# Two kinds of decode attention trade places in the mixer of a hybrid decoder step, and their cache loads with them

## The chip, the cores and the metric

The kernel runs on one core of a Trainium2 chip. The metric is device time in microseconds (us) of one launch; the number quoted is the median of the runs. The profile is one execution, recorded by the hardware profiler.

## What is computed

A two-layer decoder trunk, for a prompt of 256 tokens and, in the same launch, for 8 decode sequences of 8 new tokens each. In each layer a half-step SwiGLU FFN is followed by a mixer with three groups of heads (retention, dilated sliding window, differential attention), then cross-attention into 256 memory tokens, and a second FFN. Cut to what matters here:

```python
for l in range(DEPTH):                                     # 2 layers
    x = ffn_sublayer(x, ffn1_in[l], ffn1_out[l], ...)
    aq, ak, av, ag, bq, bk, bv, cq, ck, cv = project_mixers(x, w_in[l])
    o_a, st = retention(aq, ak, av, state_ret[:, l], pos, T)
    o_b = dilated_sample(bq, bk, bv, cache_win_k[:, l], cache_win_v[:, l], rel_bias[:, :H_B])
    past_k = cache_diff_k[page_table, l]                   # 8 pages of 128 tokens per sequence
    past_v = cache_diff_v[page_table, l]
    o_c = diff_attend(cq, concat(past_k, ck), concat(past_v, cv), pos, kpos, rel_bias[:, H_B:], lam)
    x = mixer_merge(x, o_a, ag, o_b, o_c, ...)
    x = cross_sublayer(x, cache_mem_k[:, l], cache_mem_v[:, l], ...)
    x = ffn_sublayer(x, ffn2_in[l], ffn2_out[l], ...)
```

The prompt goes through the same sublayers with its own keys and values. Differential attention forms `softmax(map 0) - lambda * softmax(map 1)`. The outputs of the window heads and of the differential heads do not depend on each other; both are needed by `mixer_merge`.

## The kernel before, in words

Everything is float32. The 320 tokens (256 prompt, 64 decode) are held with the features on the partitions. The large matmuls of the FFNs and projections run as three products each of high and low parts (lines 538 to 540 and 632 to 634); weights come through a ring of four 1 MB slots that GpSimd loads (line 485).

Attention in the mixer is a list of 16 **items**, `MIXER` (lines 54 and 55), which every engine walks in the same order. An item is one softmax: `diff_dec g` and `win_dec g` are the differential and the window heads of two decode sequences (pair g of four), `win_pro n` and `diff_pro n` are one prompt head. A decode item is always followed by a prompt item. Before, the list is `diff_dec 0, win_pro 0, ..., diff_dec 3, win_pro 3, win_dec 0, diff_pro 0, ..., win_dec 3, diff_pro 3`.

TensorE's function `attention` issues, for item i: the scores of item i+1, then the transposes of item i's probabilities (line 507), then the product with the values (`values`; line 798 for decode items). VectorE adds the bias and takes the maximum (line 1391), and scales by the sum (1428); ScalarE takes the exponential (1074) and copies the transposes out of PSUM (1084 to 1094). The scores of `diff_dec` are line 716, those of `win_dec` line 724, of the prompt items lines 732 and 733.

The cached keys and values of a decode item lie in the tile `cache`: slots 0 and 1 hold the keys of its two sequences, slots 2 and 3 the values. There is one such set, so a load waits until TensorE has used the last contents: keys wait for `s_psum` (the scores of the decode item before are done), values for `o_psum` (its value product is done). SyncE, SP in the profile, issues all of these loads in one program order (lines 365 to 467):

- A `diff_dec` item has 16 key pages and 16 value pages, each of 128 KB, each its own DMA at an address from the page table (line 378). The page numbers are first read into SP's registers (`page_numbers`, line 368).
- A `win_dec` item has two key loads and two value loads of 768 KB (line 400), a `cross_dec` item two and two of 1 MB.
- The loads of the first decode item wait only for the end of the first FFN (`w_used`), so they go out while the projections run; `cache` holds FFN weights until then.
- Behind the keys of the second decode item SP issues the outputs of the projections (`outputs_of_projections`, lines 425 and 427, 640 and 768 KB) and the load of the retention state (line 438, 1 MB).

`cache_in` makes TensorE wait for the pages: it counts the increments of `k_ready` and `v_ready`, of which there is one for each of the two sequences. After the mixer's items come retention, the output projection, the memory projections, cross-attention (items `CROSS`) and the second FFN.

Of the kernel before, what the change touches and what calls it, by code (L numbers as in the profile page):

```python
# [29 lines left out]
WK = 768  # L30
# [20 lines left out]

MIXER = ([item for i in range(4) for item in (("diff_dec", i), ("win_pro", i))]
         + [item for i in range(4) for item in (("win_dec", i), ("diff_pro", i))])
CROSS = ([("cross_dec", 0), ("cross_pro", 0)] + [("cross_dec", i) for i in (1, 2, 3)]
         + [("cross_pro", i) for i in (1, 2, 3)])
ITEMS = MIXER + CROSS
# [28 lines left out]
def build(nc, a, o):  # L87
    ctx = ExitStack()
    with ctx:
# [256 lines left out]
        def _(sp):  # L346
# [18 lines left out]
            with sp.Fori(0, L) as l:  # L365
# [14 lines left out]
                def after(kind, g):  # L380

                    return ITEMS.index((kind, g)) + 1
# [11 lines left out]

                def pair(name, used, before, g, ready, slot0, n):

                    sp.wait_ge(used.sem, used.upto(l, 0) + before)
                    for b2 in range(2):
                        src = a[name][bass.ds(l, 1), bass.ds(g * 2 + b2, 1)].rearrange("a b p c -> (a b p) c")
                        sp.dma_start(cache[:, slot0 + b2, 0:n], src).then_inc(ready[b2].sem, 16)  # L400


                def before_window(g):

                    return after("win_dec", g - 1) if g else after("diff_dec", 3)

                assert [after("cross_dec", g) for g in (1, 2)] == [len(MIXER) + 3, len(MIXER) + 4]

                def win_keys(g):
                    pair("wk", s_psum, before_window(g), g, k_ready, 0, 2 * WK)  # L410

                def win_values(g):
                    pair("wv", o_psum, before_window(g), g, v_ready, 2, 2 * WK)

                def cross_keys(g, before):
                    pair("ck", s_psum, before, g, k_ready, 0, 2048)
# [13 lines left out]
                numbers = [page_numbers(0)]  # L430

                wait_apart(sp, "sp", w_used.sem, w_used.upto(l, POS_FFN1 + FFN_SLOTS))
                diff_keys(numbers[0], 0)
                diff_values(numbers[0], 0)
                numbers += [page_numbers(1), page_numbers(2)]
                diff_keys(numbers[1], after("diff_dec", 0))
                outputs_of_projections()
                sp.dma_start(view(s_dec, [[1, 2048]]), layer_of(a["state"], l)).then_inc(st_in.sem, 16)
                diff_values(numbers[1], after("diff_dec", 0))
                diff_keys(numbers[2], after("diff_dec", 1))  # L440
                diff_values(numbers[2], after("diff_dec", 1))

                numbers.append(page_numbers(3))
                diff_keys(numbers[3], after("diff_dec", 2))
                diff_values(numbers[3], after("diff_dec", 2))
                for g in range(4):
                    win_keys(g)
                    win_values(g)
                cross_keys(0, after("win_dec", 3))
                cross_values(0, o_psum, after("win_dec", 3))  # L450
                wait_apart(sp, "sp", st_act.sem, st_act.upto(l, 1))
                sp.dma_start(layer_of(o["s_pro"], l), view(s_pro, [[1, 512]])).then_inc(out_st.sem, 16)
                sp.wait_ge(st_dve.sem, st_dve.upto(l, 4))
# [3 lines left out]
                sp.wait_ge(out_prj.sem, out_prj.upto(l, 32))  # L457
                sp.dma_start(memT, a["memT"]).then_inc(mem_in.sem, 16)
                cross_keys(1, after("cross_dec", 0))
                with sp.Fori(2, 4) as g:  # L460
                    cross_keys(g, g + (len(MIXER) + 1))
                    cross_values(g - 1, xv_psum, g - 1)
                cross_values(3, xv_psum, 3)
# [39 lines left out]
        def _(pe):  # L503
# [31 lines left out]
            with pe.Fori(0, L) as l:  # L535
# [158 lines left out]

                    return slice(64 * b2 + 32 * hp, 64 * b2 + 32 * hp + 32)

                def cache_in(ready, s, b2):

                    r = ready[b2]
                    pe.wait_ge(r.sem, r.upto(l, 16 * (NPG * min(s + 1, 4) + max(s - 3, 0))))  # L700

                def scores(i, first):
                    kind, n = ITEMS[i]
# [4 lines left out]
                    if kind == "diff_dec":  # L708
                        for c in range(3):
                            for b2, hp in QUARTERS:  # L710
                                if c == 0 and hp == 0:
                                    cache_in(k_ready, n, b2)
                                r = quarter(b2, hp)
                                rhs = (view(cache[:, b2, 1024 * c + 128 * hp:1024 * c + 128 * hp + 1], [[256, 4], [1, 128]])
                                       if c < 2 else fm[:, 6 + hp, SEQ:T])
                                last = mm(ps[r, b0 + c, 0:(512 if c < 2 else NS)],
                                          qd[:, hp, 2 * n + b2, 32 * hp:32 * hp + 32], rhs, start=True, stop=True)
                    elif kind == "win_dec":
                        for c, (at, w, bank, col) in enumerate(((0, 512, 0, 0), (512, 256, 1, 0), (0, NS, 1, 256))):
                            for b2, hp in QUARTERS:  # L720
                                if c == 0 and hp == 0:
                                    cache_in(k_ready, 4 + n, b2)
                                rhs = cache[:, b2, WK * hp + at:WK * hp + at + w] if c < 2 else fm[:, 2 + hp, SEQ:T]
                                last = mm(ps[quarter(b2, hp), b0 + bank, col:col + w], qw[:, hp, 2 * n + b2, :], rhs,
                                          start=True, stop=True)
# [8 lines left out]
                    elif kind == "cross_dec":  # L734
                        for c4 in range(4):
                            for b2, hp in QUARTERS:
                                if c4 == 0 and hp == 0:
                                    cache_in(k_ready, 8 + n, b2)
                                c = 4 * hp + c4
                                last = mm(ps[quarter(b2, hp), b0, 0:256], qc[:, c, 2 * n + b2, :],  # L740
                                          cache[:, b2, 256 * c:256 * c + 256], start=(c4 == 0), stop=(c4 == 3))
                    else:
                        for qb in range(2):
                            for c in (2 * n, 2 * n + 1):
                                last = mm(ps[:, b0, 256 * qb:256 * qb + 256], qxT[:, c, P * qb:P * qb + P], mkT[:, c, :],
                                          start=(c == 2 * n), stop=(c == 2 * n + 1))
# [33 lines left out]
                def values(i, first):  # L780
# [5 lines left out]
                    if kind in ("diff_dec", "win_dec"):  # L786
                        nk, v0 = (8, 256) if kind == "diff_dec" else (6, 0)
                        for k in range(nk + 1):
                            for b2, hp in QUARTERS:
                                if k == 0 and hp == 0:  # L790
                                    cache_in(v_ready, n if kind == "diff_dec" else 4 + n, b2)
                                r = quarter(b2, hp)
                                at = P * k + r.start
                                if k == nk:
# [14 lines left out]
                    elif kind == "cross_dec":  # L809
# [3 lines left out]
                        for kb in range(2):  # L813
                            for b2, hp in QUARTERS:
                                if kb == 0 and hp == 0:
                                    cache_in(v_ready, 8 + n, b2)
                                r = quarter(b2, hp)
                                last = mm(ps[r, bank, :], t[:, P * kb + r.start:P * kb + r.stop],  # L818
                                          cache[:, 2 + b2, 1024 * kb + 512 * hp:1024 * kb + 512 * hp + 512],
                                          start=(kb == 0), stop=(kb == 1))  # L820
# [982 lines left out]
```

## Time and profile before

| what | value |
|---|---|
| median of 3 runs | 2122.04 us (2118.92 to 2122.77) |
| the profiled execution's own time | 2125.29 us |
| its span in the profile | 2123.6 us |
| TensorE matmul busy | 1848.4 us (87%) |
| VectorE busy | 946.7 us (45%) |
| ScalarE busy | 670.3 us (32%) |
| mixer attention, layer 0, first scores to first retention transpose | 394.35 to 519.89 us |
| the same, layer 1 | 1435.57 to 1561.61 us |
| mean TensorE clock granted | 0.903 of full |

The table is read with care: TensorE's 87% is an average over FFN stages in which it never stops and attention stages in which it waits for other engines and for loads. What a change in the mixer is worth is read from the two stretches of 126 us, not from the averages.

### The profile page before, as it was taken

How to read it: one execution, taken by the hardware profiler on the slowest of the kernel's cores; microseconds unless marked ns; L12 is line 12 of the kernel's file. 1: busy time of each engine (PE TensorE's matmuls, PEld its weight loads, DVE VectorE, ACT ScalarE, POOL GpSimd, SP SyncE). 2: the span in 40 equal slices, each digit the busy share in tenths (PEclk: the TensorE clock that was granted, in tenths of full speed). 3: DMA queues.
4: the chain of work that ended last, by engine and by line, in shares of the span. 5: the costliest groups of instructions: out<-in, count | busy, mean ns of one | idle time of the engine just before them, and what ended most of it. 6: DMA issues, size and time to landing. Idle time of an engine off the chain costs nothing.

```text
span 2123.6 us, 31724 instructions
## 1 busy us (share of the span) xinstructions
PE 1848.4 (87%) x12214; PEld 1639.4 (77%) x12214; DVE 946.7 (45%) x1554; ACT 670.3 (32%) x913; POOL 114.9 (5%) x220
## 2 busy tenths in 40 slices
PE   4999999777898778999979999996788886799997
PEld 2999988535787457999969999883467773789997
DVE  3454353424454235544354543542346332545434
ACT  2333232322233124332243322432323331333323
POOL 0000100000000000000100001000000000000000
PEclk8999999866898998999979999996778988889998
DMA  5443463676143632443424434537733446224342
GB/s 176 140 157 118 147 212 130 210 234 228 65 149 108 242 116 80 157 139 129 155 91 142 158 119 162 187 127 246 249 144 106 139 139 238 80 100 151 133 137 80
DMA packets 84607, 319.51 MB, mean 150 GB/s; under 512 B 10138, under 2 KB 45338, under 8 KB 59402
## 3 DMA queue, kind: packets, MB, share of 16 engines
q0 software_dynamic: 31104, 205.53, 28.8%
q1 hardware_dynamic: 53386, 112.39, 15.3%
q8 instruction: 76, 1.25, 0.2%
q14 instruction: 41, 0.34, 0.1%
HBM read 307.10 MB, written 10.79 MB: 150 GB/s over the span
## 4 chain that ended last, share of the span: by engine, by line
PE 79%; DVE 6%; issue 4%; DMA 4%; SPq 3%; ACT 2%; DVEq 0%; ACTq 0%
PE ps L538 19%; PE ps L540 19%; PE ps L539 19%; PE ps L507 5%; SPq L378 3%; PE ps L632 3%; PE ps L634 3%; PE ps L633 3%; PE ps L798 2%; DMA cache<-in_cv 2%; DMA cache<-in_ck 2%; PE ps L740 1%; PE ps L818 1%; DVE bn L1279 1%; DMA hid<-bias_rows 1%
## 5 line engine op out<-in xcount | busy, mean ns | idle before, releaser
L538 PE MATMUL ps<-x_high,w_high 128*128 128x320 f32 x1408 | 439.7, 312 | 23.5 <-DVE w_low L1237 16.3
L539 PE MATMUL ps<-x_low,w_high 128*128 128x320 f32 x1408 | 438.8, 312 | 0.0
L540 PE MATMUL ps<-x_high,w_low 128*128 128x320 f32 x1408 | 438.6, 312 | 0.0
L985 ACT ACTIVATE w_high<-ring 128x2048 fp32r<-128x2048 f32 (+1 forms) x152 | 256.7, 1691 | 491.0 <-PE ps L540 478.6
L1237 DVE TENSOR_TENSOR w_low<-ring,w_high 128x2048 fp32r<-128x2048 f32 (+1 forms) x152 | 305.6, 2011 | 156.9 <-ACT w_high L985 156.6
L538 PEld LDWEIGHTS ps<-x_high,w_high 128*128 128x128 f32 x1408 | 267.9, 190 | 24.1 <-issue 24.1
L539 PEld LDWEIGHTS ps<-x_low,w_high 128*128 128x128 f32 x1408 | 267.9, 190 | 0.0
L540 PEld LDWEIGHTS ps<-x_high,w_low 128*128 128x128 f32 x1408 | 267.7, 190 | 0.0
L538 PE MATMUL ps<-h_high,w_high 128*128 128x320 f32 x704 | 219.9, 312 | 6.2 <-DVE h_low L1265 6.2
L1244 DVE TENSOR_TENSOR m_low<-ring,m_high 128x1024 fp32r<-128x1024 f32 x112 | 137.0, 1224 | 194.3 <-ACT m_high L1028 194.2
L485 POOL DMA_DIRECT2D ring<-in_w x216 | 114.7, 531 | 1970.7 <-PE ps L540 1769.3
L540 PE MATMUL ps<-h_high,w_low 128*128 128x320 f32 x704 | 217.5, 309 | 0.0
L539 PE MATMUL ps<-h_low,w_high 128*128 128x320 f32 x704 | 217.4, 309 | 0.0
L1028 ACT ACTIVATE m_high<-ring 128x1024 fp32r<-128x1024 f32 x112 | 118.3, 1060 | 296.5 <-PE ps L540 166.0
L1261 DVE TENSOR_TENSOR gate<-gate,ps 128x320 f32<-128x320 f32 x88 | 43.0, 489 | 274.7 <-PE ps L540 274.7
L538 PEld LDWEIGHTS ps<-h_high,w_high 128*128 128x128 f32 x704 | 132.2, 188 | 7.2 <-issue 7.2
L539 PEld LDWEIGHTS ps<-h_low,w_high 128*128 128x128 f32 x704 | 132.3, 188 | 0.0
L540 PEld LDWEIGHTS ps<-h_high,w_low 128*128 128x128 f32 x704 | 132.2, 188 | 0.0
L538 PE MATMUL ps<-x_high,m_high 128*128 128x320 f32 x384 | 126.2, 329 | 4.2 <-DVE x_low L1571 4.2
L539 PE MATMUL ps<-x_low,m_high 128*128 128x320 f32 x384 | 123.9, 323 | 0.0
L540 PE MATMUL ps<-x_high,m_low 128*128 128x320 f32 x384 | 123.6, 322 | 0.0
L507 PE MATMUL ps<-ident,tok 128*128 128x128 f32 (+1 forms) x228 | 69.0, 412 | 48.7 <-ACT tok L1042 31.5
(261 smaller groups left out, 2566.4 us busy)
## 6 DMA issues: line engine op xcount, KB each, us to landing
ring<-in_w POOLq DMA_DIRECT2D x152, 1024.0 KB, 5.2
ring<-in_w POOLq DMA_DIRECT2D x64, 704.0 KB, 4.3
cache<-in_dk SPq DMA_DIRECT2D x128, 128.0 KB, 2.3
cache<-in_dv SPq DMA_DIRECT2D x128, 128.0 KB, 2.8
cache<-in_ck SPq DMA_DIRECT2D x16, 1024.0 KB, 7.6
cache<-in_cv SPq DMA_DIRECT2D x16, 1024.0 KB, 7.5
cache<-in_wk SPq DMA_DIRECT2D x16, 768.0 KB, 7.3
cache<-in_wv SPq DMA_DIRECT2D x16, 768.0 KB, 5.0
```

The lines of the kernel that those rows point to most:

```text
L378: sp.dma_start(cache[:, slot0 + b2, 256 * pg:256 * pg + 256], src).then_inc(ready[b2].sem, 16)
L485: pool.dma_start(ring[:, r, 0:n], a[name][bass.ds(l * (a[name].shape[0] // L) + idx, 1)].rearrange("a p c -> (a p) c")).then_inc(w_ready[r ...
L507: return nc.tensor.transpose(out, in_, ident[0:in_.shape[0], 0:in_.shape[0]])
L538: mm(out, wh, xh, start=first, stop=False)
L539: mm(out, wh, xl, start=False, stop=False)
L540: return mm(out, wl, xh, start=False, stop=last)
L632: mm(out, xh, wh[:, c], start=first, stop=False)
L633: mm(out, xh, wl[:, c], start=False, stop=False)
L985: fn(w_high[:, pos % 2, 0:n], ring[:, pos % RING, 0:n], ACT.Copy).then_inc(hi_w.sem, 1)
L1028: fn(m_high[place][:, q % 2, :], ring[:, pos % RING, 1024 * (q % 2):1024 * (q % 2) + 1024], ACT.Copy)\
L1237: V.tensor_tensor(w_low[:, pos % 2, 0:n], ring[:, pos % RING, 0:n], w_high[:, pos % 2, 0:n].bitcast(F32), ALU.subtract).then_inc(lo_w.sem, 1)
L1244: V.tensor_tensor(m_low[place][:, q % 2, :], ring[:, pos % RING, 1024 * (q % 2):1024 * (q % 2) + 1024], m_high[place][:, q % 2, :].bitcast ...
```

## The change

The window items and the differential items trade places. Each decode kind now goes with its own prompt heads: `win_dec` with `win_pro` in the first half, `diff_dec` with `diff_pro` in the second. SP's loads follow: the window cache of pair 0 is loaded during the projections, and the pages of all four differential pairs come afterwards, each behind the use of the item before. The page numbers of pair g+1 are read ahead of the wait for the keys of pair g. In cross-attention a loop over two pairs on SP is written out.

```diff
-MIXER = ([item for i in range(4) for item in (("diff_dec", i), ("win_pro", i))]
-         + [item for i in range(4) for item in (("win_dec", i), ("diff_pro", i))])
+MIXER = ([item for i in range(4) for item in (("win_dec", i), ("win_pro", i))]
+         + [item for i in range(4) for item in (("diff_dec", i), ("diff_pro", i))])
...
                 def pair(name, used, before, g, ready, slot0, n):
-                    sp.wait_ge(used.sem, used.upto(l, 0) + before)
+                    if before:
+                        wait_apart(sp, "sp", used.sem, used.upto(l, before))
...
                 wait_apart(sp, "sp", w_used.sem, w_used.upto(l, POS_FFN1 + FFN_SLOTS))
-                diff_keys(numbers[0], 0)
-                diff_values(numbers[0], 0)
-                numbers += [page_numbers(1), page_numbers(2)]
-                diff_keys(numbers[1], after("diff_dec", 0))
+                win_keys(0, 0)
+                win_values(0, 0)
+                win_keys(1, after("win_dec", 0))
                 outputs_of_projections()
                 sp.dma_start(view(s_dec, [[1, 2048]]), layer_of(a["state"], l)).then_inc(st_in.sem, 16)
-                diff_values(numbers[1], after("diff_dec", 0))
-                diff_keys(numbers[2], after("diff_dec", 1))
-                diff_values(numbers[2], after("diff_dec", 1))
-
-                numbers.append(page_numbers(3))
-                diff_keys(numbers[3], after("diff_dec", 2))
-                diff_values(numbers[3], after("diff_dec", 2))
+                win_values(1, after("win_dec", 0))
+                for g in range(2, 4):
+                    win_keys(g, after("win_dec", g - 1))
+                    win_values(g, after("win_dec", g - 1))
                 for g in range(4):
-                    win_keys(g)
-                    win_values(g)
-                cross_keys(0, after("win_dec", 3))
-                cross_values(0, o_psum, after("win_dec", 3))
+                    if g < 3:
+                        numbers.append(page_numbers(g + 1))
+                    used = after("diff_dec", g - 1) if g else after("win_dec", 3)
+                    diff_keys(numbers[g], used)
+                    diff_values(numbers[g], used)
+                cross_keys(0, after("diff_dec", 3))
+                cross_values(0, o_psum, after("diff_dec", 3))
...
-                with sp.Fori(2, 4) as g:
+                for g in (2, 3):
                     cross_keys(g, g + (len(MIXER) + 1))
                     cross_values(g - 1, xv_psum, g - 1)
...
-                def cache_in(ready, s, b2):
-                    r = ready[b2]
-                    pe.wait_ge(r.sem, r.upto(l, 16 * (NPG * min(s + 1, 4) + max(s - 3, 0))))
+                def cache_in(ready, kind, n, b2):
+                    loads = {"win_dec": n + 1, "diff_dec": 4 + NPG * (n + 1), "cross_dec": 4 + 4 * NPG + n + 1}[kind]
+                    pe.wait_ge(ready[b2].sem, ready[b2].upto(l, 16 * loads))
```

How the instructions stand on SP where the mixer goes from its first half to its second (`in_dk` and `in_dv` are pages of keys and values, `in_wk` and `in_wv` the window cache; ISA rows set addresses). Before, from the last key page of pair 3 to the first window loads:

```order
L378 DMA cache<-in_dk 128x256
L378 DMA cache<-in_dv 128x256 [waits o_psum]
L378 DMA cache<-in_dv 128x256 x15
L397 REGISTER_ALU
L400 ISA [waits s_psum]
L400 DMA cache<-in_wk 128x1536
L400 ISA
L400 DMA cache<-in_wk 128x1536
L400 DMA cache<-in_wv 128x1536 [waits o_psum]
L400 DMA cache<-in_wv 128x1536
```

In the changed program, from the last window loads to the first key pages:

```order
L401 DMA cache<-in_wv 128x1536 [waits o_psum]
L401 DMA cache<-in_wv 128x1536
L368 TENSOR_LOAD pt x2
L331 REGISTER_ALU
L378 ISA [waits s_psum]
L378 DMA cache<-in_dk 128x256
L378 ISA
L378 DMA cache<-in_dk 128x256
```

All sixteen key pages of pair 0 now stand behind a wait for the scores of `win_dec 3`, and the reading of pair 1's page numbers stands ahead of them; before, only four large loads stood at this place.

TensorE at the same place (`qd` and `qw` are the queries of the differential and window decode heads, `arena` the transposed probabilities, `hid` here the new tokens' values, `fm` their keys). Before:

```order
L798 MATMUL ps<-cache,arena 32x128 x29
L798 MATMUL ps<-hid,arena 32x128 x4
L700 REGISTER_ALU [waits m_done]
L724 MATMUL ps<-cache,qw 32x512 [waits k_ready0]
L724 MATMUL ps<-cache,qw 32x512
L724 MATMUL ps<-cache,qw 32x512 [waits k_ready1]
```

Changed:

```order
L792 MATMUL ps<-cache,arena 32x128 x21
L792 MATMUL ps<-hid,arena 32x128 x4
L694 REGISTER_ALU [waits m_done]
L710 MATMUL ps<-cache,qd 32x512 [waits k_ready0]
L710 MATMUL ps<-cache,qd 32x512
L710 MATMUL ps<-cache,qd 32x512 [waits k_ready1]
```

The first scores of the second half now wait for pages (`k_ready`), where they waited for two window loads. Lines of TensorE's part stand six lower in the changed file.

## Rows read from the trace of the kernel before

**Rows 1.** The page, the chain that ended last: shares by engine and by line.

```profile
PE 79%; DVE 6%; issue 4%; DMA 4%; SPq 3%; ACT 2%; DVEq 0%; ACTq 0%
PE ps L538 19%; PE ps L540 19%; PE ps L539 19%; PE ps L507 5%; SPq L378 3%; PE ps L632 3%; PE ps L634 3%; PE ps L633 3%; PE ps L798 2%; DMA cache<-in_cv 2%; DMA cache<-in_ck 2%; PE ps L740 1%; PE ps L818 1%; DVE bn L1279 1%; DMA hid<-bias_rows 1%
```

**Rows 2.** Timeline of SP, layer 0: start us, us for the whole row, line, count.

```profile
284.27 9.79 SPq L378 DMA_DIRECT2D cache<-in_dk  x16
...
396.70 9.30 SPq L378 DMA_DIRECT2D cache<-in_dk  x16
...
409.76 9.84 SPq L378 DMA_DIRECT2D cache<-in_dv  x16
420.03 9.73 SPq L378 DMA_DIRECT2D cache<-in_dk  x16
429.94 7.45 SPq L378 DMA_DIRECT2D cache<-in_dv  x16
438.90 10.12 SPq L378 DMA_DIRECT2D cache<-in_dk  x16
...
501.92 0.81 SPq L400 DMA_DIRECT2D cache<-in_wv  x2
503.58 0.85 SPq L400 DMA_DIRECT2D cache<-in_ck  x2
```

**Rows 3.** Timeline of TensorE, layer 0: start, us, line, [idle before <-what ended it].

```profile
394.35 1.92 PE L716 MATMUL ps<-cache,qd 128*32 128x512 f32 x16 [2.17 <-DVE hid L1351]
...
409.48 1.93 PE L716 MATMUL ps<-cache,qd 128*32 128x512 f32 x14
...
431.78 2.77 PE L716 MATMUL ps<-cache,qd 128*32 128x512 f32 x10 [3.25 <-DMA cache<-in_dk]
...
448.87 1.77 PE L716 MATMUL ps<-cache,qd 128*32 128x512 f32 x4
450.84 1.48 PE L716 MATMUL ps<-cache,qd 128*32 128x512 f32 x10 [0.20 <-DMA cache<-in_dk]
...
466.11 2.12 PE L724 MATMUL ps<-cache,qw 128*32 128x512 f32 x16
...
501.77 1.50 PE L724 MATMUL ps<-cache,qw 128*32 128x512 f32 x16
...
519.89 0.48 PE L507 MATMUL ps<-ident,hid 128*128 128x128 f32 x1 [0.38 <-DVE tok L1464]
```

**Rows 4.** Timeline of SP, layer 1: its three key loads inside the mixer.

```profile
1438.56 8.82 SPq L378 DMA_DIRECT2D cache<-in_dk  x16
...
1461.05 10.39 SPq L378 DMA_DIRECT2D cache<-in_dk  x16
...
1480.57 10.24 SPq L378 DMA_DIRECT2D cache<-in_dk  x16
```

**Rows 5.** Timeline of TensorE, layer 1.

```profile
1435.57 2.48 PE L716 MATMUL ps<-cache,qd 128*32 128x512 f32 x16 [2.17 <-DVE hid L1351]
...
1507.95 1.74 PE L724 MATMUL ps<-cache,qw 128*32 128x512 f32 x16
...
1516.33 2.66 PE L798 MATMUL ps<-cache,arena 128*32 128x128 f32 x48 [0.63 <-ACT arena L1091]
...
1519.28 1.50 PE L724 MATMUL ps<-cache,qw 128*32 128x512 f32 x16
...
1543.18 1.69 PE L724 MATMUL ps<-cache,qw 128*32 128x512 f32 x12
...
1561.61 0.69 PE L507 MATMUL ps<-ident,hid 128*128 128x128 f32 x2 [0.39 <-DVE tok L1464]
```

**Rows 6.** Windows, layer 0: last three columns granted clock, DMA share, GB/s.

```profile
412.00:416.00 4.00, 2.14 (x11) 1.17 (x11) 2.80 (x9) 1.79 (x3) 0.00 (x0) 1.00 0.98 364
...
428.00:432.00 4.00, 0.75 (x8) 0.20 (x8) 0.00 (x0) 0.00 (x0) 0.00 (x0) 0.73 0.85 238
...
504.00:508.00 4.00, 2.53 (x20) 1.89 (x21) 2.82 (x14) 1.47 (x3) 0.00 (x0) 1.00 1.02 420
```

More of the change, by code:

```diff
@@ L400, in pair, with win_keys, win_values @@
                         sp.dma_start(cache[:, slot0 + b2, 0:n], src).then_inc(ready[b2].sem, 16)
[L403 to L413, printed above, removed]
+                def win_keys(g, before):
+                    pair("wk", s_psum, before, g, k_ready, 0, 2 * WK)
+                def win_values(g, before):
+                    pair("wv", o_psum, before, g, v_ready, 2, 2 * WK)
                 def cross_keys(g, before):
@@ L711, in scores @@
                                 if c == 0 and hp == 0:
-                                    cache_in(k_ready, n, b2)
+                                    cache_in(k_ready, kind, n, b2)
                                 r = quarter(b2, hp)
@@ L721, in scores @@
                                 if c == 0 and hp == 0:
-                                    cache_in(k_ready, 4 + n, b2)
+                                    cache_in(k_ready, kind, n, b2)
                                 rhs = cache[:, b2, WK * hp + at:WK * hp + at + w] if c < 2 else fm[:, 2 + hp, SEQ:T]
@@ L737, in scores @@
                                 if c4 == 0 and hp == 0:
-                                    cache_in(k_ready, 8 + n, b2)
+                                    cache_in(k_ready, kind, n, b2)
                                 c = 4 * hp + c4
@@ L790, in values @@
                                 if k == 0 and hp == 0:
-                                    cache_in(v_ready, n if kind == "diff_dec" else 4 + n, b2)
+                                    cache_in(v_ready, kind, n, b2)
                                 r = quarter(b2, hp)
@@ L815, in values @@
                                 if kb == 0 and hp == 0:
-                                    cache_in(v_ready, 8 + n, b2)
+                                    cache_in(v_ready, kind, n, b2)
                                 r = quarter(b2, hp)
```

## The prediction, made before the changed kernel ran

> **What bounds the kernel now.** I read the chain of waits first [rows 1]: 79% of it is TensorE, nearly all in the FFN and projection lines 538 to 540 and 632 to 634, which the change doesn't touch. The page loads stand in it as SP's own issue, line 378, with 3%. So the question is confined to the two stretches of mixer attention, of which I read SP's timeline beside TensorE's.
>
> Layer 0's stretch lasts from 394.35 to 519.89, 125.54 us; layer 1's from 1435.57 to 1561.61, 126.04 us; mean 125.8 [rows 3, 5]. I call the start of a decode item's scores S, and the moment at which TensorE may go on because the second sequence's key pages are in, R.
>
> In the first half SP is the bound. It issues the 16 value pages of one pair in 7.45 us, then the 16 key pages of the next in about 10, and 2.0 us after the last key page TensorE goes on: keys end at 420.03 + 9.73 = 429.76, R is 431.78, after an idle time of 3.25 us [rows 2, 3]. The next R comes 19.06 us later, at 450.84. The same item with little stall needs 450.84 to 466.11, 15.27 us, to the next decode item. In the second half a window pair lasts (501.77 - 466.11) / 3 = 11.89 us in layer 0 and (1543.18 - 1507.95) / 3 = 11.74 us in layer 1 [rows 3, 5], and there the bound is the walk from score to maximum, exponential, transposes, copies and values, since four large loads take SP only about 1.7 us a pair (two of them 0.81 us) [rows 2].
>
> One point matters more than the rest: pair 0's pages were loaded at 284.27, 110 us before their use [rows 2]. Only three of four differential pairs waited.
>
> **The change part by part.** *Removed and added work:* none on TensorE, VectorE or ScalarE; the items are the same sixteen in another order. SP's loads are the same too. The written-out loop in cross-attention removes a branch that stands between loads and waits for TensorE; I cost it at nothing, hidden by those waits, and at 1 us in all if it were not.
>
> *Window pairs first.* The pair that follows a window *prompt* item is the one in layer 1 that takes 1519.28 - 1507.95 = 11.33 us [rows 5]; later ones, behind a differential prompt item with twice the maxima and exponentials, take about 0.4 more. All window pairs now have that neighbour: 3 x 11.33 = 34.0 us. Ends: 33.5 (the first pair has nothing before it) and 35.7 (3 x 11.89).
>
> *From the last window scores to the first R.* SP issues the last window values 0.15 us after S and takes 0.81 [rows 2, 3]. Then come page numbers: where SP read them between values and keys, the gap is 438.90 - (429.94 + 7.45) = 1.51 us [rows 2]. Then 16 key pages; the six such rows inside the mixer are 9.30, 9.73, 10.12, 8.82, 10.39 and 10.24, mean 9.77 [rows 2, 4]; then 2.02 us to land. 0.15 + 0.81 + 1.51 + 9.77 + 2.02 = 14.3 us. The wait for `s_psum` of `win_dec 3` is over before: the loads behind it went out at S + 1.81 (503.58) [rows 2, 3]. This load was covered, and is not any more; TensorE would have been ready after 11.33, so 2.9 us of stall are new.
>
> *R to R.* The values wait for the product before, which is done by then, so SP runs through: 0.18 us gap (429.76 to 429.94), values 7.45, numbers 1.51, keys 9.77, in all 18.9 us, twice (pairs 1 and 2). For pair 3 no numbers are read and the gap is 0.43 (419.60 to 420.03), 17.8 us. TensorE needs 15.27, or 448.87 - 431.78 = 17.09 where the stall before left its clock low (0.73 mean granted in that window, levels 1.2 and 2.4 GHz) [rows 3, 6]; both lie under 17.8, so SP stays the bound and the low clock is hidden, except in the last pair. The value load of 9.84 us at 409.76 is the far end; I take 7.45, because the slow one ran beside the projections' outputs and the state load, which now go out in the window half.
>
> *Last R to the end.* 15.27 for the last differential pair, and what a last pair costs over a middle one: 519.89 - 501.77 - 11.89 = 6.2 in layer 0, 1561.61 - 1543.18 - 11.74 = 6.7 in layer 1, taken as 6.45. Together 21.7 us; with a low clock 23.5.
>
> *Weighing a rule on size.* Sixteen pages of 128 KB are issued in 8.8 to 10.4 us and land 2 us later, at 238 GB/s [rows 2, 4, 6]. The Trainium skill, "DMA: Bandwidth & Descriptors", section Bandwidth, puts a 64 KB transfer at 0.95 us and asks for 1 MiB per DMA; taken as one page after the other, 16 pages would need over 15.2 us, and the now exposed loads would cost some 45 us more in each layer. The trace disagrees: the pages overlap.
>
> **The sum**, for one layer: 34.0 + 14.3 + 37.8 + 17.8 + 21.7 = 125.6 us, against 125.8. That is -0.2 a layer, -0.4 in all. The profiled execution took 2125.29 us and would take 2124.9. The median of the runs, 2122.04, lies 3.25 under it, so I predict **2121.6 us**. The new stall of pair 0 (2.9) and page numbers read inside two more gaps are paid for by the window pairs' shorter walk, by value pages that no longer share the queue with 2.5 MB of outputs and state (2.4 us of issue), and by the end.
>
> Below about 0.2%, 4.2 us, a measurement of this kernel can't tell from no change.
>
> **The rivals.**
>
> *The keys go out faster (faster).* If all four key loads take 8.82 us, as the quickest row [rows 4], instead of 9.77, each layer gains 3.8 us: 2121.6 - 7.6 = 2114.0. For it: both quick rows, 8.82 and 9.30, had no value load right before them, and pair 0's keys won't either. Against: pairs 1 to 3 do have one, and such rows are 9.73 to 10.39. Under 8.82 nothing in the trace reaches. It counts as faster when the mean falls below about 9.3.
>
> *The lost cover is not given back (slower).* SP's first 32 page loads leave the projections for a place where TensorE waits for them, the window pairs stay at 11.8 (+1.4 a layer), and keys behind values take 10.39 (+2.5): 125.6 + 3.9 = 129.5, 3.7 over before in each layer, 2129.4. For it: three of the four rows behind values are above 10. Against: the 11.33 row, and the quick rows for pair 0. It decides when the two together cost over 2.3 us a layer. The Trainium skill says the same of such a move in "DMA: Bandwidth & Descriptors", Rules for kernel authors: issue a DMA early, compute, and wait for it late. By that rule the group with most DMAs should keep the early place; the trace agrees as far as pair 0 of before shows no wait.
>
> *The window half starves (slower).* Behind `win_dec 1`'s keys SP now has outputs and state in its queue, and the window values behind them. From about 396.1 that is 1.57 + 2.49 + 1.57 = 5.6 MB, needed 8.4 us after the second S (1516.33 - 1507.95) [rows 5], at 394.35 + 11.33 + 8.4 = 414.1. At the 238 GB/s of page traffic it would be 5.7 us late, 2121.6 + 11.4 = 2133.0 for both layers; it decides below 5.6 / 18.0 = 313 GB/s. Large loads moved 420 GB/s and the mixed traffic with outputs in it 364 [rows 6], so it is unlikely; loads of weights still running at the start speak for it.
>
> That the change does nothing is excluded: the order shown above has it on every engine.
>
> **How the numbers follow.** No change 0.64, keys faster 0.16, lost cover 0.12, starving 0.08. Only these give the chances: faster 0.16, same 0.64, slower 0.20. The range reaches from the quick keys' 2114 to just over the lost cover, 2130; it leaves out the starving case, and value loads that all stay at 9.84 (+14.3). The forecast's own range is 2118 to 2126, which holds the ends of the window pairs, a low clock in the last pair (+1.8 a layer), and keys half way to either end.
>
> **What would show it.** Right: in the changed profile the first window pairs 11.3 to 11.5 us apart with no wait for `in_wk` or `in_wv`; the first `diff_dec` scores with a wait for `in_dk` of about 3 us, R's 18.9, 18.9 and 17.8 apart; four waits for keys a layer where there were three; SP's line 378 still in the chain, and with more than 3%. From the last window scores to the end it is 91.6 us, against 34.0 before them. Wrong: key rows far from 9.8; a value load over 8 us in the differential half; a wait for a window load; R to R set by TensorE and not by SP; any change outside the two stretches above 1 us, since I cost everything there at nothing.

## The result, and the profile after

The changed kernel takes 2132.08 us (median of 6 runs, 2127.56 to 2134.16), the kernel before on the same chip 2120.88 (6 runs, 2118.92 to 2126.08). The ratio is 1.0036, with a 95% interval from 1.0023 to 1.0050: slower by 5 to 11 us, where 2121.6 had been predicted. The two medians themselves lie 11.2 us apart, a ratio of 1.0053, so the size of the loss is less sure than the interval says. A later repetition of both gave 1.0025 (1.0013 to 1.0037) and 2131.51 against 2125.72, 5.8 us. By the two ratios the loss is 5 to 8 us, and I reckon with that.

The profiled execution took 2133.52 us, its span is 2131.8. Page of the changed kernel, busy times, then the chain by engine and line, then two rows of its DMA issues (count, KB each, us to landing):

```profile
PE 1853.9 (87%) x12214; PEld 1640.3 (77%) x12214; DVE 947.1 (44%) x1554; ACT 670.5 (31%) x913; POOL 114.4 (5%) x220
...
PE 78%; DVE 6%; SPq 5%; DMA 5%; issue 4%; ACT 2%; DVEq 0%; ACTq 0%
PE ps L532 19%; PE ps L534 19%; PE ps L533 19%; PE ps L501 5%; SPq L378 4%; PE ps L626 3%; PE ps L627 3%; PE ps L628 3%; DMA cache<-in_ck 2%; PE ps L792 1%; PE ps L734 1%; DMA cache<-in_cv 1%; DVE bn L1273 1%; PE ps L812 1%; DMA hid<-bias_rows 1%
...
cache<-in_dk SPq DMA_DIRECT2D x128, 128.0 KB, 2.4
cache<-in_dv SPq DMA_DIRECT2D x128, 128.0 KB, 2.4
```

The work is the same as before; what grew in the chain is SP's own issue, from 3% to 5%, line 378 within it from 3% to 4% [rows 1].

Timeline of SP, changed kernel, layer 0. These rows answer to [rows 2]:

```profile
401.93 1.39 SPq L432 DMA_DIRECT2D s_dec<-in_state  x1
408.82 1.73 SPq L401 DMA_DIRECT2D cache<-in_wv  x2
...
432.85 0.81 SPq L401 DMA_DIRECT2D cache<-in_wv  x2
435.21 10.19 SPq L378 DMA_DIRECT2D cache<-in_dk  x16
445.58 7.45 SPq L378 DMA_DIRECT2D cache<-in_dv  x16
454.53 9.97 SPq L378 DMA_DIRECT2D cache<-in_dk  x16
464.68 7.45 SPq L378 DMA_DIRECT2D cache<-in_dv  x16
473.64 9.89 SPq L378 DMA_DIRECT2D cache<-in_dk  x16
483.71 7.75 SPq L378 DMA_DIRECT2D cache<-in_dv  x16
491.84 9.18 SPq L378 DMA_DIRECT2D cache<-in_dk  x16
```

Timeline of TensorE in the same stretch, for [rows 3]; line 718 is the window scores, 710 the differential ones:

```profile
396.75 1.50 PE L718 MATMUL ps<-cache,qw 128*32 128x512 f32 x16 [2.14 <-DVE hid L1345]
...
432.59 1.50 PE L718 MATMUL ps<-cache,qw 128*32 128x512 f32 x16
...
444.22 1.86 PE L710 MATMUL ps<-cache,qd 128*32 128x512 f32 x4
447.26 1.48 PE L710 MATMUL ps<-cache,qd 128*32 128x512 f32 x10 [1.18 <-DMA cache<-in_dk]
...
466.26 2.71 PE L710 MATMUL ps<-cache,qd 128*32 128x512 f32 x10 [2.86 <-DMA cache<-in_dk]
...
485.34 1.48 PE L710 MATMUL ps<-cache,qd 128*32 128x512 f32 x10 [0.98 <-DMA cache<-in_dk]
...
502.89 1.48 PE L710 MATMUL ps<-cache,qd 128*32 128x512 f32 x10 [1.67 <-DMA cache<-in_dk]
...
523.28 1.97 PE L501 MATMUL ps<-ident,hid 128*128 128x128 f32 x8 [0.39 <-DVE tok L1458]
```

In layer 0 all four differential pairs now wait for keys, with SP running through from 435.21 to the end. Before, only two pairs did, not three as the prediction says: pair 1's scores start at 409.48 without a wait [rows 3]. What came late for that pair were its values (kernel before, TensorE, layer 0):

```profile
422.63 3.63 PE L798 MATMUL ps<-cache,arena 128*32 128x128 f32 x60 [0.95 <-DMA cache<-in_dv]
```

In layer 1 of the changed kernel three pairs show such a wait. There is also one that before did not have, for window keys (for [rows 5]):

```profile
1438.05 1.74 PE L718 MATMUL ps<-cache,qw 128*32 128x512 f32 x16 [2.17 <-DVE hid L1345]
...
1460.84 1.05 PE L718 MATMUL ps<-cache,qw 128*32 128x512 f32 x4 [0.55 <-DMA cache<-in_wk]
1462.90 1.80 PE L718 MATMUL ps<-cache,qw 128*32 128x512 f32 x8 [1.01 <-DMA cache<-in_wk]
...
1476.19 1.73 PE L718 MATMUL ps<-cache,qw 128*32 128x512 f32 x16
...
1490.61 2.78 PE L710 MATMUL ps<-cache,qd 128*32 128x512 f32 x10 [2.07 <-DMA cache<-in_dk]
...
1567.58 1.97 PE L501 MATMUL ps<-ident,hid 128*128 128x128 f32 x8 [0.39 <-DVE tok L1458]
```

The repetition has no wait for window keys in either layer, so this one belongs to a single execution. It also shows three waits for keys in each layer.

Where the time went, by stages, from the first and last rows of each stage (us; "mixer" is first scores to first retention transpose, "rest" from there to the first cross-attention scores: retention, output projection, memory projections). Under each kernel stands a second profiled execution with the same mixer, from the runs below:

| | mixer 0 | mixer 1 | rest 0 | rest 1 |
|---|---|---|---|---|
| before | 125.54 | 126.04 | 178.65 | 178.04 |
| before, cross loop written out | 125.32 | 122.19 | 178.52 | 178.38 |
| changed | 126.53 | 129.53 | 177.70 | 177.88 |
| changed, repeated | 126.85 | 128.52 | 178.32 | 179.63 |

The four mixers of before average 124.8 us, the four of the changed kernel 127.9: 3.1 a layer, 6.2 in all, which lies between the 5.3 and 7.6 us of the two ratios. Everything else stays within what two executions of one kernel differ by. In the first pair of profiles another 4.7 us lie at the two ends of the launch (first FFN matmul at 47.29 instead of 44.83, and the second layer's last FFN 2.3 longer). The repetition starts at 44.94 and takes 307.44 us for that last FFN; before has 44.83 and 307.40. So that part belongs to the execution and not to the change.

### The profile page after: what moved, and what is told of

Its sections match the earlier page's. It is cut to its first block, busy times and chain, and to the rows that moved or that the text cites. A ratio compares the mean times of both kernels' runs of the same rounds, so it can differ in the third digit from the quotient of the medians.

```text
span 2131.8 us, 31734 instructions
## 1 busy us (share of the span) xinstructions
PE 1853.9 (87%) x12214; PEld 1640.3 (77%) x12214; DVE 947.1 (44%) x1554; ACT 670.5 (31%) x913; POOL 114.4 (5%) x220
## 4 chain that ended last, share of the span: by engine, by line
PE 78%; DVE 6%; SPq 5%; DMA 5%; issue 4%; ACT 2%; DVEq 0%; ACTq 0%
PE ps L532 19%; PE ps L534 19%; PE ps L533 19%; PE ps L501 5%; SPq L378 4%; PE ps L626 3%; PE ps L627 3%; PE ps L628 3%; DMA cache<-in_ck 2%; PE ps L792 1%; PE ps L734 1%; DMA cache<-in_cv 1%; DVE bn L1273 1%; PE ps L812 1%; DMA hid<-bias_rows 1%
## 5 line engine op out<-in xcount | busy, mean ns | idle before, releaser
L532 PE MATMUL ps<-x_high,w_high 128*128 128x320 f32 x1408 | 440.1, 313 | 23.9 <-DVE w_low L1231 16.7
```

Source lines behind the costliest of these rows:

```text
L532: mm(out, wh, xh, start=first, stop=False)
```

## The experiments

In each the ratio is to the kernel before on the same chip, with its 95% interval. A "mixer" figure is the mean of the two layers' stretches in that run's profile.

**1. Is the written-out cross loop free?** The kernel before with this alone:

```diff
-                with sp.Fori(2, 4) as g:
+                for g in (2, 3):
```

> The kernel before, with only the loop over pairs 2 and 3 of SP's cross-attention loads written out. Theory A (the loss arises in the mixer, from the page loads and the window half): no difference from the kernel before, within 2 us, and cross-attention, from its first scores to its last value product on cached values, stays at 51.2 to 51.9 us. Theory B (the written-out loop is a part of the loss, by its longer straight code on SP): 2 to 5 us slower than before, with later issues of in_ck or in_cv in cross-attention.

Measured 0.9994 (0.9984 to 1.0004), 2124.79 us against 2124.74. It costs at most 1 us, so the loss lies in the order and the loads that go with it. Layer 1's mixer, 122.19 against 126.04 in the kernel before, shows that one and the same mixer spreads by 4 us between layers and executions, so one profile is a weak base for a few microseconds.

**2. The changed kernel once more, and with the outputs out of the window half.** The state load moves with the outputs behind the last value pages:

```diff
-                outputs_of_projections()
-                sp.dma_start(view(s_dec, [[1, 2048]]), layer_of(a["state"], l)).then_inc(st_in.sem, 16)
                 win_values(1, after("win_dec", 0))
...
                     diff_values(numbers[g], used)
+                outputs_of_projections()
+                sp.dma_start(view(s_dec, [[1, 2048]]), layer_of(a["state"], l)).then_inc(st_in.sem, 16)
                 cross_keys(0, after("diff_dec", 3))
```

> The changed kernel, with the outputs of the projections and the state load moved from behind the second window keys to behind the last value pages. Theory A (in the changed kernel the window half starves behind these 2.5 MB, 2.6 us in the profiled layer 1): no wait for in_wk in either layer, window half 35.5 to 36 us in both, 2 to 5 us faster than the changed kernel. Theory C (the starving is a chance of one execution, and the loss is the page loads that are no longer covered): within 1.5 us of the changed kernel.

> The changed kernel once more, for a second profile and to be timed on one chip with the next two. If the starving of the window half is part of what the change does (theory A): a wait for in_wk of 1 to 3 us in at least one of the two layers again, window halves of 36 to 38 us, mixers of 126 to 130 us, and a ratio to the kernel before of 1.002 to 1.005. If it was a chance of one execution (theory C): no such wait.

> e2 once more, beside the changed kernel on the same chip. Theory A (outputs and state ahead of the window loads cost time): 3 to 6 us faster than e9, and no wait for in_wk in either layer. Theory C: within 1.5 us of e9; the difference between e2 and the changed kernel was one between two sets of runs.

Outputs late: 1.0007 (0.9995 to 1.0020), and on the second chip 1.0016 (1.0002 to 1.0029), where the changed kernel had 1.0025 (1.0013 to 1.0037). The intervals overlap, so a gain in time is not shown. What moved inside is clearer. Windows over the first to the fourth window scores, changed kernel; last three columns granted clock, DMA share, GB/s:

```profile
396.75:432.59 35.84, 25.21 (x288) 15.49 (x288) 11.45 (x46) 10.25 (x29) 0.00 (x0) 0.76 0.84 318
1438.05:1476.19 38.14, 27.01 (x288) 15.58 (x288) 11.44 (x46) 10.26 (x29) 0.00 (x0) 0.74 0.80 299
```

The same with outputs late:

```profile
396.43:432.07 35.64, 25.82 (x287) 15.47 (x288) 11.44 (x46) 10.27 (x29) 0.00 (x0) 0.71 0.66 250
1441.13:1475.69 34.56, 24.76 (x288) 14.93 (x288) 11.44 (x46) 10.27 (x29) 0.00 (x0) 0.76 0.69 257
```

Over both executions of each, the three pairs take 35.84, 38.14, 35.43, 36.48 (mean 36.5) with the outputs among them and 35.64, 34.56, 35.59, 34.90 (mean 35.2) without. So outputs and state load cost about 1.3 us a layer there. It is a rough figure: half of it is the one stretch of 38.14 us with the wait for window keys, and without that one the changed kernel's mean is 35.9. The mixer as a whole did not gain: 127.9 and 127.8 against 127.9, because the differential half behind it took 1.4 us longer, above all its last pair (mean of four 24.7, against 23.2). That is where the transfers were moved to, but TensorE shows no wait for them there, so why it is longer is open.

**3. Neighbours alone.** The order of the decode kinds as before, but each with its own prompt heads:

```diff
-MIXER = ([item for i in range(4) for item in (("diff_dec", i), ("win_pro", i))]
-         + [item for i in range(4) for item in (("win_dec", i), ("diff_pro", i))])
+MIXER = ([item for i in range(4) for item in (("diff_dec", i), ("diff_pro", i))]
+         + [item for i in range(4) for item in (("win_dec", i), ("win_pro", i))])
```

> The kernel before, with the differential decode heads still first and their page loads unchanged, but each kind beside its own prompt heads (diff_dec with diff_pro, then win_dec with win_pro). Theory A (the neighbour costs or gives nothing; what counts is which pages have cover): within 2 us of the kernel before, window pairs 11.8 to 12.0 us as with either neighbour. My prediction's term (a window pair is 11.33 us beside window prompt heads): window pairs 11.3 to 11.5, and 2 to 4 us faster than before.

> e3 once more. If matching neighbours give their gain in the mixer: mixers of 120 to 122.5 us again, against 122 to 126 of the two profiles with crossed neighbours, and 9 to 12 us faster than the kernel before. If the gain in the mixer was a chance of the granted clock: a mixer over 124 us in one layer at least, and a smaller gain in time.

Measured 0.9945 (0.9931 to 0.9959) and 0.9960 (0.9942 to 0.9979): 8 to 12 us faster than the kernel before. Expected were 2 to 4 us, if anything. Two gains of like size make this up. The mixers take 121.4 and 122.1, some 3 us less a layer: the differential half lasts as long as before although its prompt items are the heavier ones (72.35 and 70.03 us here, 71.76 and 72.38 before), since SP's issue sets it, and the window half's pairs carry the lighter ones. The second gain lies where nothing was edited, in the stage behind the mixer (175.6 to 175.9 instead of 178.0 to 178.7). Windows over the output and memory projections, layer 0, of the kernel before, of the changed kernel and of this one:

```profile
563.70:698.50 134.80, 122.11 (x720) 112.03 (x720) 61.57 (x72) 46.84 (x70) 7.94 (x15) 0.89 0.35 118
```

```profile
566.70:701.00 134.30, 121.60 (x723) 111.61 (x724) 61.52 (x72) 46.87 (x70) 7.91 (x15) 0.89 0.34 118
```

```profile
559.70:691.60 131.90, 119.17 (x723) 109.24 (x723) 61.56 (x72) 46.91 (x70) 7.95 (x15) 0.91 0.35 120
```

The same work, DVE and ACT to 0.1 us, in 2.4 to 2.9 us less at a granted clock of 0.91 instead of 0.89. More on it at the end.

**4. Outputs late in the kernel before.** The same two statements moved behind the last window values:

> The kernel before, with the outputs of the projections and the state load moved from behind the second key pages to behind the last window values. Theory A (SP's issue is the bound of the page half, and value pages issued beside these transfers took 9.4 to 9.8 us where 7.45 is the rule): the second value load takes 7.5 us, starts no later, so the third key load ends about 2 us sooner in each layer, and the kernel is 3 to 5 us faster than before. Rival (the wait moves on: the saved time is given back as a longer wait at the next pages): within 1.5 us.

Measured 0.9989 (0.9977 to 1.0000); the edit frees the second value load, which goes from 9.84 to 7.98 us of issue, and the mixers take 125.7 and 123.0 (mean 124.4, before 124.8). From the first scores to the keys of pair 3 a layer is 1.2 us ahead (55.3 instead of 56.5), and at the end of the mixer 0.4 are left, less than mixers of one kernel differ by. So the 2.4 us of issue that my sum took as a gain of the move are not seen in the mixer even in the order of before.

**5. Order alone, neighbours crossed as before.** The changed kernel with

```diff
-MIXER = ([item for i in range(4) for item in (("win_dec", i), ("win_pro", i))]
-         + [item for i in range(4) for item in (("diff_dec", i), ("diff_pro", i))])
+MIXER = ([item for i in range(4) for item in (("win_dec", i), ("diff_pro", i))]
+         + [item for i in range(4) for item in (("diff_dec", i), ("win_pro", i))])
```

> The changed kernel with the prompt heads of the two halves exchanged: win_dec beside diff_pro first, diff_dec beside win_pro after. The change is two changes: the order of the decode kinds (with their loads), and the neighbours. Theory A (the two add up: matching neighbours give about 10 us, as e3 had it, and the order takes about 18): about 18 us slower than the kernel before, 1.007 to 1.010 of it, and mixers of about 130 us. Theory B (they do not add up; the order alone costs what the changed kernel shows, and matching gives something only where window pairs come last): within 3 us of the changed kernel, 1.002 to 1.005.

Measured 1.0029 (1.0015 to 1.0043), 2130.02 against 2123.85, mixers 127.8. With the neighbour runs it fills a square (ratio, and mean mixer in us):

| | neighbours crossed | own neighbours |
|---|---|---|
| differential first | 1 (124.8) | 0.9945, 0.9960 (121.7) |
| window first | 1.0029 (127.8) | 1.0036, 1.0025 (127.9) |

The order costs 6 us with crossed neighbours and 14 to 19 with own ones (the medians on the chip that ran both, 2131.51 and 2115.01, are 16.5 apart). Own neighbours gain 8 to 12 us if the window half comes last and nothing if it comes first. Why is not shown. One would say that a heavy prompt item behind the last differential pair has no page wait left to hide in. But that pair takes 24.67 and 23.91 us here with a light prompt item beside it, and 21.94 to 25.26 (mean 23.2) in the changed kernel with a heavy one.

**6. Give pair 0 its cover back.** One differential pair first, then four window pairs, then the other three; all with own neighbours, loads in that order:

```diff
-MIXER = ([item for i in range(4) for item in (("win_dec", i), ("win_pro", i))]
-         + [item for i in range(4) for item in (("diff_dec", i), ("diff_pro", i))])
+MIXER = ([("diff_dec", 0), ("diff_pro", 0)]
+         + [item for i in range(4) for item in (("win_dec", i), ("win_pro", i))]
+         + [item for i in (1, 2, 3) for item in (("diff_dec", i), ("diff_pro", i))])
```

> The changed kernel with differential pair 0 moved to the front, where its pages are loaded during the projections; then the four window pairs, then differential pairs 1 to 3, and matching neighbours throughout. Theory A (the loss of the order is the one page load that lost its cover, and the window loads queued behind outputs and state): three waits for keys a layer instead of four, mixers 3 to 5 us shorter than in the changed kernel, 6 to 9 us faster in all. Theory C (the order costs because the differential pair stands last, and its longer last pair has nothing behind it): three waits instead of four, but the time within 3 us of the changed kernel.

Measured 0.9983 (0.9968 to 0.9997), mixers 122.8 and 122.4. Against the changed kernel that is 5.3 us a layer and 9 to 11 us of time, for moving one pair with its loads. Timeline of TensorE, layer 0:

```profile
394.80 2.40 PE L712 MATMUL ps<-cache,qd 128*32 128x512 f32 x16 [2.14 <-DVE hid L1347]
...
460.23 1.48 PE L712 MATMUL ps<-cache,qd 128*32 128x512 f32 x10 [1.52 <-DMA cache<-in_dk]
...
479.58 2.78 PE L712 MATMUL ps<-cache,qd 128*32 128x512 f32 x10 [3.67 <-DMA cache<-in_dk]
...
497.23 1.48 PE L712 MATMUL ps<-cache,qd 128*32 128x512 f32 x10 [0.16 <-DMA cache<-in_dk]
...
517.57 1.97 PE L503 MATMUL ps<-ident,hid 128*128 128x128 f32 x8 [0.38 <-DVE tok L1460]
```

The first row has all sixteen matmuls in one piece: its pages were there. The 5.3 divide as follows, by the starts of scores. Pair 0 to the next item: 15.43 instead of 17.57, 19.13, 19.07 and 18.00 (mean 18.4), 3.0 us. The last three differential pairs to the end: 59.9 instead of 61.4, 1.5. The rest, 0.8, is the window half.

**7. In turns.** `diff_dec, diff_pro, win_dec, win_pro`, four times:

> Differential and window pairs take turns (diff_dec, diff_pro, win_dec, win_pro), so that SP has about 28 us for the 32 pages and four window loads of a turn. If SP's issue is the bound of the page half: R to R is no longer 18.9 us; from window scores to the next R 13.4 us (0.15 + 0.2 + 1.6 until the scores are done, 9.8 issue, 2.0 landing), from R to the window scores 15.3 to 16, a turn 29 to 30 where before it was 31 (19.1 + 11.9), so 1 to 2 us less for each of three turns a layer: 3 to 10 us faster than the kernel before. Rival (the waits only move, the window keys come behind 16 value pages and are late at 15.3 us): waits for in_wk in every turn, no gain over e3 and none over before.

Measured 0.9967 (0.9952 to 0.9981), mixers 121.0 and 120.9. Each differential pair's pages now have a window pair to hide behind, though not wholly: in layer 0 pairs 2 and 3 still wait 1.97 and 1.22 us for keys. It is faster than the kernel before, and not told apart from experiment 3.

**8. Is SP's issue the bound of the page half?** Experiment 3, with GpSimd's queue issuing the value pages of the second sequence of pairs 1 to 3 (a semaphore of their own, `v_pool`), placed in the middle of the weight loads:

```diff
+                        for g in (1, 2, 3):
...
+                            wait_apart(pool, "pool", o_psum.sem, o_psum.upto(l, ITEMS.index(("diff_dec", g - 1)) + 1))
+                            for pg in range(NPG):
+                                src = a["dv"][bass.ds(nums[pg], 1), bass.ds(l, 1)].rearrange("a b p c -> (a b p) c")
+                                pool.dma_start(cache[:, 3, 256 * pg:256 * pg + 256], src).then_inc(v_pool.sem, 16)
```

> e3 (differential pairs first, matching neighbours), and GpSimd, idle there, issues the value pages of the second sequence of pairs 1 to 3; SP issues 24 pages a pair instead of 32. If SP's issue of about 17.5 us a pair is the bound of the page half: the distance from R to R falls by the 3.7 us of eight value pages, to the 15.3 to 16 us that TensorE's walk takes, and the kernel is 8 to 16 us faster than e3. Rival (the transfers themselves are the bound, at about 240 GB/s of page traffic, or the slower start of GpSimd's DMAs makes the values late): R to R stays above 17.5 us or a wait for in_dv takes the place of the one for in_dk, and the time is within 4 us of e3.

Measured 0.9934 (0.9910 to 0.9957), 2109.15 against 2123.85; mixers 118.2 and 118.1, 3.5 less than in experiment 3. Timeline of SP, layer 0:

```profile
396.44 9.06 SPq L379 DMA_DIRECT2D cache<-in_dk  x16
409.59 4.36 SPq L396 DMA_DIRECT2D cache<-in_dv  x8
414.75 8.82 SPq L379 DMA_DIRECT2D cache<-in_dk  x16
426.39 3.66 SPq L396 DMA_DIRECT2D cache<-in_dv  x8
431.59 8.83 SPq L379 DMA_DIRECT2D cache<-in_dk  x16
```

Timeline of TensorE there:

```profile
428.30 1.48 PE L749 MATMUL ps<-cache,qd 128*32 128x512 f32 x10 [0.66 <-DMA cache<-in_dk]
...
443.65 2.25 PE L749 MATMUL ps<-cache,qd 128*32 128x512 f32 x16
...
460.30 1.94 PE L757 MATMUL ps<-cache,qw 128*32 128x512 f32 x16
```

Same bytes, half the value pages on another queue, and the spacing falls from 19 to 15.4 us, which is the item's own 15.27, and to 16.7 for the last pair. So the page half was bound by the issue on one queue and not by bandwidth. Some waits for pages remain: pair 1's values come 1.88 us late in layer 0 and the last pair's 0.73. In time it has the lowest median of all kernels tried here, but it had been expected 8 to 16 us faster than experiment 3, and the ratios differ by 2 to 6 us. Its interval overlaps that of experiment 3, so the step from there is shown in the mixers, not in the total.

## Why the prediction was wrong

**What held.** The differential half was right term by term. From the last window scores to the first R, 14.3 predicted: 447.26 - 432.59 = 14.67 and 1490.61 - 1476.19 = 14.42. R to R, 18.9, 18.9, 17.8 predicted: 19.00, 19.08, 17.55 in layer 0. From the last R to the end, 21.7 predicted: 523.28 - 502.89 = 20.4, in the repetition 21.5. All value loads of this half take 7.45 to 7.75, the key loads of both layers 9.18 to 10.19, mean 9.83 against 9.77; SP stayed the bound. The first R to the end is 76.0 and 77.0 us against a sum of 77.3. Nor did anything outside the two stretches change by more than executions of one kernel differ by, though that alone is over the 1 us that I had allowed. The count of waits was misread: before, two pairs a layer waited for keys and not three. The sum doesn't use it.

**The step that failed: "All window pairs now have that neighbour: 3 x 11.33 = 34.0 us."** They took 36.5 in the mean, even above my upper end of 35.7, 2.5 more a layer. The 11.33 came from one row, and I laid it to the neighbour alone. The corresponding pair took 11.76 in layer 0 of the same profile, and 11.36 and 9.78 in experiment 1, at the same place and with the same neighbour. I picked the quicker of two and built a mechanism on it. In experiment 5 the first three window pairs have differential prompt items beside them and take 35.7 and 36.0 us, no longer than in the changed kernel, so in this place the neighbour gave nothing. What does go with most of a pair's length is the granted clock (third column from the end). Kernel before, both layers:

```profile
466.11:477.87 11.76, 8.73 (x106) 5.13 (x102) 4.92 (x21) 4.46 (x14) 0.00 (x0) 0.80 0.69 269
1507.95:1519.28 11.33, 8.27 (x107) 5.01 (x103) 4.92 (x21) 4.46 (x14) 0.00 (x0) 0.83 0.70 279
```

Experiment 1, layer 1, with the differential prompt item beside the pair, then experiment 3, layer 0, with the window one; in both a window prompt item stands before the pair:

```profile
1508.71:1518.49 9.78, 6.76 (x107) 4.08 (x103) 4.93 (x21) 4.46 (x14) 0.00 (x0) 1.00 0.82 322
478.25:488.04 9.79, 6.75 (x103) 4.08 (x99) 4.27 (x17) 3.59 (x10) 0.00 (x0) 1.00 0.83 321
```

At a clock of 1.00 the pair takes 9.8 us whichever stands beside it. Between the row of 11.33 and the one of 9.78 TensorE's own busy time falls from 8.27 to 6.76 us (first column behind the length), as much as the pair's length, with VectorE and ScalarE the same. Further rows of these three runs have 11.3 to 11.6 us at 0.81 to 0.83 and 12.2 to 12.5 at 0.75 or 0.76. In experiment 3 the pairs behind a window prompt item are quicker (9.8 to 11.6) than the first one behind a differential item (11.6 to 12.6), as the prediction had it, but in experiment 8 they are not (11.7 to 12.1 against 11.6 and 12.2). What makes the clock rise at one pair and not at the next, no run took apart. The parts that the runs do show are a pair of about 11.7 us (35.2 for three in the runs with outputs late), and about 1.3 us of traffic: the outputs and the state load, which I had removed from the differential half for a gain and put into the window half for nothing. There the traffic is 318 and 299 GB/s, at the 313 that I had named as the point from which the starving decides, and layer 1 has the short wait for `in_wk`. That rival's mechanism is there at a quarter of its size: the stretch is 1.3 us longer, not 5.7.

**The base was a microsecond high.** I compared with 125.8, the mean of two mixers in one profile; four mixers average 124.8. With the 2.5 above, less 0.2 in the rest of the sum, this makes the 3.3 us a layer between the predicted -0.2 and the measured +3.1. Twice that is 6.6 of the 10.5 us between 2121.6 and the first median of 2132.08. The rest lies outside the mixers or in the spread of the executions, and isn't explained; against the ratios of 1.0025 and 1.0036 hardly anything is left.

**The rivals.** "The lost cover is not given back", 2129.4, was the nearest: its window pairs at 11.8 came, its keys at 10.39 behind values did not. Experiment 6 gives its stall the size that I had priced, 3.0 against 2.9, but shows that with what follows from it the cover is worth 5.3 us a layer. It was given 0.12. The Trainium skill, "DMA: Bandwidth & Descriptors", Rules for kernel authors, says to issue a DMA early, compute, and wait for it late; by that the group of 32 page loads belongs in the early place. Here the trace agrees, with 15.43 us for a covered pair 0 and 18.4 for an uncovered one. "The keys go out faster" came nowhere in the changed kernel. In experiment 8 the keys inside the mixer took 8.8 to 9.1, where only half of the value pages stood before them.

**What the sum hid.** It came out at -0.2 because a loss that was certain (2.9 of stall, plus 1.5 of page numbers in each of two more gaps) was set against gains each of which hung on one row. Experiment 4 shows that of the largest, the value load at 7.45 instead of 9.84, the mixer keeps nothing that can be told from its spread. That the new place of the outputs would cost something was seen, and priced at nothing.

## What to carry to other kernels

When one queue's issue bounds a phase, give the place whose loads are covered by earlier work to the group with the most DMAs, put the heavy neighbours beside the work that waits for loads, and end with a group that waits for nothing; here that was worth some 16 us between two orders of the same sixteen items (some 12 of them in the mixers), and a second queue for a quarter of the pages took another 3.5 us from each mixer. Do not take a pair's duration from its quickest row: two layers and two executions of one mixer gave 9.8 to 11.8 us for one and the same pair. Read the granted clock beside each row that you take as a price. And when DMAs leave one phase for another, price them where they arrive.

## What the runs showed that was not expected

The output and memory projections behind retention, untouched by any edit, take two lengths. The difference lies between their first product and the start of their last block of products (the 31.1 to 31.6 us behind that are alike in all). In the 16 layers with `diff_pro` as the mixer's last item (before, changed twice, and experiments 1, 2 twice, 4 and 6) this part takes 103.0 to 103.5 us at a granted clock of 0.88, with one exception of 100.9. In all 10 layers with `win_pro` last (experiments 3 twice, 5, 7, 8) it takes 100.3 to 101.9 at 0.90 or 0.91. The exception, layer 1 of the repeated changed kernel, follows a retention of 47.15 us instead of some 43.6; but layer 1 of experiment 4 has 46.1 there and still takes 103.5. So the levels of 1.2 and 2.4 GHz are dealt out differently some 40 to 150 us after the mixer has ended. Why the last item should decide it is open: no run took it apart. It makes about half of experiment 3's gain, and in layers of experiments 5, 7 and 8 it was taken back by that longer stretch ahead of it (rest 179.5 to 180.0).

The start of the launch differs by up to 2.8 us between executions with the same instructions (first FFN matmul at 44.49 to 47.29), and this alone makes 2.5 of the 8.2 us between the spans of the first pair of profiles.

Not tried: the page numbers of all pairs read ahead of the differential half. An estimate: the gaps between values and keys are 1.5 us with the reading in them and 0.4 without, so it could take 1.1 us out of each of two such gaps, and as much ahead of the first pair's keys.
